# A chunked mLSTM stage worked by single heads, and by pairs of heads in row and column groups of TensorE

## The chip, the cores and the metric

The kernel runs on one core of one Trainium2 chip. The metric is the device time of one execution in microseconds; three runs of the kernel before are shown, and one further execution was profiled. The engines are TensorE (PE, with its weight loads shown apart as PEld), VectorE (DVE), ScalarE (ACT), GpSimd (POOL) and SyncE (SP). TensorE's granted clock is shown as a share of 2.4 GHz, so 0.50 is 1.2 GHz.

## The reference, cut to what matters

The whole kernel is a small network: adaptive normalisation, a token mixer (an mLSTM in both directions beside a convolution), mixture-of-experts layers, attention and a state-space part. The change touches one stage, the recurrent part of the mLSTM. For each chunk of 128 tokens, each direction and each of 4 heads (key width 64, value width 128) it computes

```
# boundary states, one chunk after the other
C_new = a * C + e * (w * v)^T k            # n is carried as a 129th column of v
# outputs of a chunk
s   = (q k^T) * exp(log_d - m_t)           # log_d is -inf above (or below) the diagonal
num = s v + e_int * (C q)
den = sum(s) + e_int * (n q)
h   = num / max(|den|, exp(-m_t))
```

There are 10 chunks in each direction: 2 of context, of which only the states are wanted, and 8 of the sequence. The two directions' h are added.

## The kernel before, in words

`stage_gates` leaves, for each of the 80 columns (10 chunks j, 2 directions d, 4 heads h), the gate sums and maxima as 128-token columns (`E`, `EI`, `EN`, `WS`, `EA`) and the negated running maxima turned to rows in `NMT` (80 x 128). Then `stage_mlstm` runs as one block, between two barriers of all engines. Its work list is `units`, one unit for each (j, d, h), 80 in all. All but the last 8 move a state (72 units), and all but the first 16 give an output (64 units, numbered v).

For one unit with an output the engines do this:

- POOL (L793): `wv`, the values weighted by `WS`, two buffers.
- TensorE, in this order: the local state (L821, `k_tok` 64 columns wide, into PSUM partitions 0-63 or 64-127 by the head's parity, banks 4 and 5 in turn), the state's product with q (L830, contraction over 64 rows), the value product (L833, 128 x 128 by 129), and then for the unit two further on the scores q k^T (L804, 64 rows) and a one-hot product that spreads that unit's row of `NMT` over all partitions (L808, 80 rows).
- DVE: for the unit one further on, `dec` = that spread row + `E` + mask (L864) and, after ACT's exponential, `pt` = scores x `dec` (L871); for this unit the sum `hsum` of the two products (L883), three instructions on one column for the denominator (L886, L888, L889), the scaled output (L894, or L896 where it is added to the other direction's) and the state's update (L900).
- ACT: the exponential (L842) and `inter`, the state's product scaled by `EI` (L852).

All operands are fp32. Each fp32 matmul shows in the trace as two loads and two matmul records. The order on each engine is the order in which the code is written; semaphores between the engines are waited for in that order. The waits that the change touches are these lines:

```
if u >= 2:
    pe.wait_ge(state_moved, u - 1)      # before the local product of unit u: two banks
...
if v >= 2:
    pe.wait_ge(pt_ready, v - 1)         # before scores(v), which run two units ahead
```

Of the kernel before, what the change touches and what calls it, by code (L numbers as in the profile page):

```python
# [108 lines left out]
def sem(s, name):  # L109
    s.sems.append(s.nc.alloc_semaphore(name))  # L110
    return s.sems[-1]
# [643 lines left out]
def stage_mlstm(s):  # L755


    nc = s.nc
    units = [(j, d, h) for j in range(STEPS) for d in range(2) for h in range(H1)]
    U0 = NC * 2 * H1  # L760
    US = (STEPS - 1) * 2 * H1
    NV = len(units) - U0
    W = DV + 1
    s.h = s.x[:, 0:NT // 2, :].rearrange("p t (a n) -> p (t a) n", a=2)
    out_unit = lambda v: units[U0 + v]
    tile_of = lambda j, d: bwd_tile(j) if d else fwd_tile(j)
    with nc.sbuf_tensor("neg_mask", [P, 2, P], F32) as neg_mask, \
            nc.sbuf_tensor("dec", [P, 2, P], F32) as dec, nc.sbuf_tensor("pt", [P, 2, P], F32) as pt, \
            nc.sbuf_tensor("wv", [P, 2, W], F32) as wv, nc.sbuf_tensor("c_state", [P, 2, 2, W], F32) as state, \
            nc.sbuf_tensor("inter", [P, 2, W], F32) as inter, nc.sbuf_tensor("hsum", [P, 2, W], F32) as hsum, \  # L770
            nc.sbuf_tensor("dn", [P, 2, 2], F32) as dn:
        masks_set, scores_done, dec_ready, exp_ready, pt_ready = (sem(s, f"m_{x}") for x in ("masks_set", "scores_done", "dec_ready", "exp_ready", "pt_ready"))
        wv_ready, local_done, state_moved = (sem(s, f"m_{x}") for x in ("wv_ready", "local_done", "state_moved"))
        num_done, inter_ready, combined = (sem(s, f"m_{x}") for x in ("num_done", "inter_ready", "combined"))

        def lanes(h):
            return slice((h % 2) * DK, (h % 2) * DK + DK)

        with nc.Block() as block:
            @block.gpsimd  # L780
            def _(pool):
                c = s.pool_c
                c.link(pool, pool.memset(neg_mask[:, :, :], 0.0))

                pool.affine_select(out=neg_mask[:, 0, :], in_=neg_mask[:, 0, :], compare_op=ALU.is_ge, fill=NEG,
                                   base=0, pattern=[[1, P]], channel_multiplier=-1).then_inc(masks_set, 1)
                pool.affine_select(out=neg_mask[:, 1, :], in_=neg_mask[:, 1, :], compare_op=ALU.is_ge, fill=NEG,
                                   base=0, pattern=[[-1, P]], channel_multiplier=1).then_inc(masks_set, 1)
                for u, (j, d, h) in enumerate(units):
                    if u < US:  # L790
                        if u >= 2:
                            pool.wait_ge(local_done, u - 1)
                        pool.tensor_scalar(wv[:, u % 2, :], s.v_aug[:, tile_of(j, d), h, :], s.WS[:, j, d, h:h + 1],  # L793
                                           None, ALU.mult).then_inc(wv_ready, 1)

            @block.tensor
            def _(pe):
                def scores(v):
                    j, d, h = out_unit(v)
                    t0 = tile_of(j, d) * P  # L800
                    if v >= 2:
                        pe.wait_ge(pt_ready, v - 1)
                    bank = s.bank[v % 2]
                    pe.matmul(bank[:, 0:P], s.qkT[lanes(h), 2 + h // 2, t0:t0 + P], s.qkT[lanes(h), h // 2, t0:t0 + P],  # L804
                              start=True, stop=True)
                    r = (j * 2 + d) * H1 + h

                    pe.matmul(bank[:, P:2 * P], s.ident[0:NCOL, r:r + 1].to_broadcast([NCOL, P]), s.NMT[:, :],  # L808
                              start=True, stop=True).then_inc(scores_done, 1)

                for u, (j, d, h) in enumerate(units):
                    v = u - U0
                    if v == -2:
                        scores(0)
                    if v == -1:
                        scores(1)
                    if u < US:
                        pe.wait_ge(wv_ready, u + 1)
                        if u >= 2:
                            pe.wait_ge(state_moved, u - 1)  # L820
                        pe.matmul(s.bank[4 + u % 2][lanes(h), 0:W], s.k_tok[:, tile_of(j, d), h * DK:(h + 1) * DK],  # L821
                                  wv[:, u % 2, :], start=True, stop=True).then_inc(local_done, 1)
                    if v >= 0:
                        t0 = tile_of(j, d) * P
                        bank = s.bank[2 + v % 2]
                        if v >= 2:
                            pe.wait_ge(combined, v - 1)

                        pe.wait_ge(state_moved, u - 2 * H1 + 1)
                        pe.matmul(bank[:, 256:256 + W], s.qkT[lanes(h), h // 2, t0:t0 + P], state[lanes(h), d, h // 2, :],  # L830
                                  start=True, stop=True)
                        pe.wait_ge(pt_ready, v + 1)
                        pe.matmul(bank[:, 0:W], pt[:, v % 2, :], s.v_aug[:, tile_of(j, d), h, :],  # L833
                                  start=True, stop=True).then_inc(num_done, 1)
                        if v + 2 < NV:
                            scores(v + 2)

            @block.scalar
            def _(act):
                def exp(v):  # L840
                    act.wait_ge(dec_ready, v + 1)
                    act.activation(dec[:, v % 2, :], dec[:, v % 2, :], ACT.Exp).then_inc(exp_ready, 1)  # L842

                for u, (j, d, h) in enumerate(units):
                    v = u - U0
                    if 0 <= v + 1 < NV:
                        exp(v + 1)
                    if v >= 0:
                        act.wait_ge(num_done, v + 1)
                        if v >= 2:  # L850
                            act.wait_ge(combined, v - 1)
                        act.activation(inter[:, v % 2, :], s.bank[2 + v % 2][:, 256:256 + W], ACT.Copy,  # L852
                                       scale=s.EI[:, j, d, h:h + 1]).then_inc(inter_ready, 1)

            @block.vector
            def _(dve):
                c = s.dve_c
                c.link(dve, dve.memset(state[:, :, :, :], 0.0))
                dve.wait_ge(masks_set, 2)

                def decay(v):
                    j, d, h = out_unit(v)
                    dve.wait_ge(scores_done, v + 1)
                    dve.scalar_tensor_tensor(dec[:, v % 2, :], s.bank[v % 2][:, P:2 * P], s.E[:, j, d, h:h + 1],  # L864
                                             neg_mask[:, d, :], ALU.add, ALU.add).then_inc(dec_ready, 1)

                def weights(v):
                    dve.wait_ge(exp_ready, v + 1)
                    if v >= 2:
                        dve.wait_ge(num_done, v - 1)  # L870
                    dve.tensor_tensor(pt[:, v % 2, :], s.bank[v % 2][:, 0:P], dec[:, v % 2, :], ALU.mult).then_inc(pt_ready, 1)  # L871

                for u, (j, d, h) in enumerate(units):
                    v = u - U0
                    if 0 <= v + 1 < NV:
                        decay(v + 1)
                    if 0 <= v + 1 < NV:
                        weights(v + 1)
                    if v >= 0:
                        dve.wait_ge(inter_ready, v + 1)  # L880
                        H = hsum[:, v % 2, :]

                        dve.tensor_tensor(H, s.bank[2 + v % 2][:, 0:W], inter[:, v % 2, :], ALU.add).then_inc(combined, 1)  # L883
                        dve.wait_ge(combined, v + 1)

                        c.link(dve, dve.tensor_scalar(dn[:, v % 2, 0:1], H[:, DV:W], -1.0, s.EN[:, j, d, h:h + 1],  # L886
                                                      ALU.mult, ALU.max))
                        c.link(dve, dve.tensor_tensor(dn[:, v % 2, 0:1], dn[:, v % 2, 0:1], H[:, DV:W], ALU.max))  # L888
                        c.link(dve, dve.reciprocal(dn[:, v % 2, 1:2], dn[:, v % 2, 0:1]))  # L889
                        t = tile_of(j, d)  # L890
                        to = s.h[:, t, h * DV:(h + 1) * DV]
                        first = j < (bwd_tile(t) if not d else t + NC)
                        if first:
                            c.then(dve.tensor_scalar(to, H[:, 0:DV], dn[:, v % 2, 1:2], None, ALU.mult))  # L894
                        else:
                            c.then(dve.scalar_tensor_tensor(to, H[:, 0:DV], dn[:, v % 2, 1:2], to, ALU.mult, ALU.add))  # L896
                    if u < US:
                        dve.wait_ge(local_done, u + 1)
                        C = state[lanes(h), d, h // 2, :]
                        dve.scalar_tensor_tensor(C, C, s.EA[lanes(h), j, d, h:h + 1], s.bank[4 + u % 2][lanes(h), 0:W],  # L900
                                                 ALU.mult, ALU.add).then_inc(state_moved, 1)


# [2263 lines left out]
```

## Time and profile before

| | |
|---|---|
| three runs | 3322.37, 3321.8, 3315.33 us; median 3321.8 |
| the profiled execution | 3317.97 us, of which the span is 3316.2 us |
| the stage's first product and last output | 453.05 us and 685.79 us after the span's start |
| mean granted clock over the span | 0.904 |

A time in the trace is counted from the span's start. A line such as `562.35 0.80 PE L830 MATMUL ... x2` gives the start, the stretch that the records cover, the engine, the line of the kernel and the number of records. What follows in brackets is idle time of that engine just before, and what ended it. Matmuls are pipelined and their ends are modelled, so the spacing of starts tells more than the durations.

### The profile page before, as it was taken

How to read it: one execution, taken by the hardware profiler on the slowest of the kernel's cores; microseconds unless marked ns; L12 is line 12 of the kernel's file. 1: busy time of each engine (PE TensorE's matmuls, PEld its weight loads, DVE VectorE, ACT ScalarE, POOL GpSimd, SP SyncE). 2: the span in 40 equal slices, each digit the busy share in tenths (PEclk: the TensorE clock that was granted, in tenths of full speed). 3: DMA queues.
4: the chain of work that ended last, by engine and by line, in shares of the span. 5: the costliest groups of instructions: out<-in, count | busy, mean ns of one | idle time of the engine just before them, and what ended most of it. 6: DMA issues, size and time to landing. Idle time of an engine off the chain costs nothing. (4 is left out here: it accounts for less than half of the span.)

```text
span 3316.2 us, 39108 instructions
## 1 busy us (share of the span) xinstructions
PE 2861.8 (86%) x12086; PEld 2025.9 (61%) x12087; DVE 1726.0 (52%) x2710; ACT 1168.1 (35%) x1598; POOL 840.4 (25%) x1036
## 2 busy tenths in 40 slices
PE   4999969968787999999999993998987999883897
PEld 4455446647536777777777772446664666673776
DVE  3667845556535556756666554036644111435653
ACT  1100011123205556656666553005513111213653
POOL 0100021122173333333343332038320000103333
PEclk9999955569798999999999996999998999986999
DMA  5321100003316878978888865300011111316873
GB/s 217 103 102 54 54 0 1 1 29 142 152 65 226 276 225 271 316 252 300 306 274 295 249 165 168 113 0 1 27 15 51 38 44 33 135 70 223 306 232 59
DMA packets 159184, 463.49 MB, mean 140 GB/s; under 512 B 37964, under 2 KB 67264, under 8 KB 138328
## 3 DMA queue, kind: packets, MB, share of 16 engines
q1 hardware_dynamic: 115816, 358.12, 29.2%
q0 software_dynamic: 43264, 104.02, 13.1%
q8 instruction: 60, 0.98, 0.1%
q14 instruction: 44, 0.36, 0.0%
HBM read 414.31 MB, written 91.62 MB: 153 GB/s over the span
## 5 line engine op out<-in xcount | busy, mean ns | idle before, releaser
L1829 DVE TENSOR_TENSOR moe_low<-moe_raw,moe_high 128x2048 fp32r<-128x2048 f32 x160 | 359.5, 2288 | 80.6 <-ACT moe_high L1774 80.6
L1739 PE MATMUL psum<-moe_high,moe_xg_high 128*128 128x512 f32 x960 | 389.9, 406 | 6.1 <-issue 3.1
L1741 PE MATMUL psum<-moe_high,moe_xg_low 128*128 128x512 f32 x960 | 378.3, 394 | 0.0
L1740 PE MATMUL psum<-moe_low,moe_xg_high 128*128 128x512 f32 x960 | 375.5, 391 | 0.0
L1774 ACT ACTIVATE moe_high<-moe_raw 128x2048 fp32r<-128x2048 f32 x160 | 297.5, 1914 | 0.1
L1675 POOL DMA_INDIRECT moe_acc<-moe_y_blk,moe_is_now x97 | 216.2, 2229 | 303.6 <-DMA moe_acc<-moe_y_blk,moe_is_now 273.0
L1786 ACT ACTIVATE moe_y_blk<-psum,row_w 128x1024 f32 x124 | 138.1, 1113 | 232.7 <-DMA moe_acc<-moe_y_blk,moe_is_now 129.1
L1726 PE MATMUL psum<-moe_high_down,moe_hid_high 128*128 x488 | 208.3, 427 | 12.7 <-DVE moe_hid_low L1838 12.6
L1713 PE MATMUL psum<-ident,moe_xg 128*128 128x128 f32 x976 | 132.5, 280 | 96.8 <-DMA moe_xg<-moe_rows,moe_ig_now 96.8
L1739 PEld LDWEIGHTS psum<-moe_high,moe_xg_high 128*128 128x128 f32 x960 | 181.7, 189 | 43.1 <-issue 4.8
L1741 PEld LDWEIGHTS psum<-moe_high,moe_xg_low 128*128 128x128 f32 x960 | 180.8, 188 | 43.1
L1740 PEld LDWEIGHTS psum<-moe_low,moe_xg_high 128*128 128x128 f32 x960 | 181.7, 189 | 36.0
L1834 DVE TENSOR_TENSOR moe_xg_low<-psum,moe_xg_high 128x512 fp32r<-128x512 f32 x244 | 157.4, 685 | 82.6 <-ACT moe_xg_high L1780 82.4
L1728 PE MATMUL psum<-moe_high_down,moe_hid_low 128*128 x488 | 196.6, 403 | 0.0
L1727 PE MATMUL psum<-moe_low,moe_hid_high 128*128 x488 | 196.3, 402 | 0.0
L1713 PEld LDWEIGHTS psum<-ident,moe_xg 128*128 128x128 f32 x976 | 111.6, 143 | 128.6 <-DMA moe_xg<-moe_rows,moe_ig_now 119.9
L1829 DVE TENSOR_TENSOR moe_low<-moe_raw,moe_high_down 128x2048 fp32r<-128x2048 f32 x80 | 182.7, 2284 | 0.0
L2300 PE MATMUL psum<-w_ring,hT 128*128 128x512 f32 x384 | 167.1, 598 | 9.2 <-DMA w_ring<-in_w_in 9.2
L502 PE MATMUL psum<-hT,w_ring 128*128 128x512 f32 x384 | 168.8, 599 | 1.1 <-PEq L344 1.1
L1780 ACT ACTIVATE moe_xg_high<-psum 128x512 fp32r<-128x512 f32 x244 | 133.3, 596 | 85.2 <-PE psum L1713 81.4
L1838 DVE TENSOR_TENSOR moe_hid_low<-psum,moe_hid_high 128x256 fp32r<-128x256 f32 x122 | 51.2, 420 | 210.7 <-ACT moe_hid_high L1791 210.6
L1665 POOL DMA_INDIRECT moe_xg<-moe_rows,moe_ig_now x122 | 132.6, 1087 | 107.4 <-POOL moe_ig_now L1662 99.9
(574 smaller groups left out, 5305.3 us busy)
## 6 DMA issues: line engine op xcount, KB each, us to landing
moe_raw<-in_we_gate SPq DMA_DIRECT2D x64, 1024.0 KB, 7.7
moe_raw<-in_we_up SPq DMA_DIRECT2D x64, 1024.0 KB, 11.4
moe_raw<-in_we_down SPq DMA_DIRECT2D x64, 1024.0 KB, 7.5
moe_raw<-in_w_e_gate SPq DMA_DIRECT2D x16, 1024.0 KB, 7.0
moe_raw<-in_w_e_up SPq DMA_DIRECT2D x16, 1024.0 KB, 10.1
moe_raw<-in_w_e_down SPq DMA_DIRECT2D x16, 1024.0 KB, 8.7
w_ring<-in_w_in SPq DMA_DIRECT2D x12, 1024.0 KB, 7.3
wada<-in_w_ada SPq DMA_DIRECT2D x8, 1024.0 KB, 10.5
```

Source lines behind the costliest of these rows:

```text
L502: last = pe.matmul(bank[:, 0:width], w[:, k, c0:c0 + P], h[:, k, :], start=(k == 0), stop=(k == KD - 1))
L1675: pool.indirect_dma_start(mo.acc, bass.IndirectOffsetOnAxis(ap=is_now[q][:, 0:1], axis=0), y_blk[:, q * D:(q + 1) * D], None, bounds_check ...
L1713: last = pe.transpose(bx[k // 4][:, (k % 4) * P:(k % 4 + 1) * P], xg[:, k * P:(k + 1) * P], s.ident[:, :])
L1726: pe.matmul(by[n][:, :], R(hid_high[:, f, :]), w_hi, start=(f == 0), stop=False)
L1727: pe.matmul(by[n][:, :], R(hid_high[:, f, :]), w_lo, start=False, stop=False)
L1728: last = pe.matmul(by[n][:, :], R(hid_low[:, f, :]), w_hi, start=False, stop=(f == KF - 1))
L1739: pe.matmul(to, x_hi, R(of_k(w_hi, k)), start=(k == 0), stop=False)
L1740: pe.matmul(to, x_hi, R(of_k(w_lo, k)), start=False, stop=False)
L1741: last = pe.matmul(to, x_lo, R(of_k(w_hi, k)), start=False, stop=(k == KD - 1))
L1774: act.activation(R(high[:, at:at + 2048]), raw[r][:, part], ACT.Copy).then_inc(w_high, 1)
L1829: dve.tensor_tensor(R(low[:, at:at + 2048]), raw[r][:, part], hi, ALU.subtract).then_inc(w_low, 1)
L2300: last = pe.matmul(s.bank[i % 4], s.hT[:, k, t * P:(t + 1) * P], ring[:, g % 2, k, :], start=(k == 0), stop=(k == KD - 1))
```

## The change

The work list becomes `pairs`: one entry for each (j, d, k), where k stands for heads 2k and 2k+1, 40 in all; 36 move states (`PS`) and 32 give outputs (`NV`, numbered v from pair `P0` = 8 on). For a pair TensorE issues two local products into the two halves of one bank (bank 7), two products with the state from rows 0-63 and 64-127 into two banks, two value products, and two score products likewise from the two row halves. The spread of the maxima is made once for two pairs (`maxima(g)`: one matmul, 80 rows by 512 columns, from a table `NM4` that holds `NMT` four times, each with the rows of one head alone). The chain of DVE and ACT is widened: one mask addition of 512 columns for four heads, one `pt` of 256, one `hsum` of 258, denominators of 2 columns, one state update of 128 partitions; `E` goes into the exponential as its bias. Scores run one pair ahead, where they ran two units ahead.

```
-    units = [(j, d, h) for j in range(STEPS) for d in range(2) for h in range(H1)]
+    pairs = [(j, d, k) for j in range(STEPS) for d in range(2) for k in range(H1 // 2)]
+    P0 = NC * H1
+    PS = (STEPS - 1) * H1
+    NV = len(pairs) - P0
...
+        both = lambda first: s.psum[:, first * 512:(first + 2) * 512].rearrange("p (i n) -> p i n", i=2)
+        out_banks = lambda v: 2 + 2 * (v % 2)
...
+                for p, (j, d, k) in enumerate(pairs[:PS]):
+                    if p >= 2:
+                        pool.wait_ge(local_done, p - 1)
+                    for i in range(2):
+                        h = 2 * k + i
+                        pool.tensor_scalar(wv[:, p % 2, i, :], s.v_aug[:, tile_of(j, d), h, :], s.WS[:, j, d, h:h + 1],
                                            None, ALU.mult).then_inc(wv_ready, 1)
...
+                def maxima(g):
+
+                    pe.matmul(s.bank[6][:, :], of_group[:, NC * 2 + g:NC * 2 + g + 1].to_broadcast([NCOL, P]), NM4[:, :, :],
+                              start=True, stop=True).then_inc(maxima_done, 1)
+
                 def scores(v):
...
-                    if v >= 2:
-                        pe.wait_ge(pt_ready, v - 1)
...
+                    for i in range(2):
+                        last = pe.matmul(s.bank[i][:, 0:P], s.qkT[lanes(i), 2 + k, t0:t0 + P], s.qkT[lanes(i), k, t0:t0 + P],
+                                         start=True, stop=True)
+                    last.then_inc(scores_done, 1)
+
+                for p, (j, d, k) in enumerate(pairs):
+                    v = p - P0
+                    if v == -1:
+                        pe.wait_ge(maxima_set, 1)
+                        maxima(0)
                         scores(0)
...
+                    if p < PS:
+                        pe.wait_ge(wv_ready, 2 * (p + 1))
+                        if p >= 1:
+                            pe.wait_ge(state_moved, p)
+                        for i in range(2):
+                            h = 2 * k + i
+                            last = pe.matmul(s.bank[7][lanes(i), 0:W], s.k_tok[:, tile_of(j, d), h * DK:(h + 1) * DK],
+                                             wv[:, p % 2, i, :], start=True, stop=True)
+                        last.then_inc(local_done, 1)
                     if v >= 0:
...
+                        pe.wait_ge(state_moved, p - H1 + 1)
+                        for i in range(2):
+                            pe.matmul(s.bank[bank + i][:, 256:256 + W], s.qkT[lanes(i), k, t0:t0 + P], state[lanes(i), d, k, :],
+                                      start=True, stop=True)
                         pe.wait_ge(pt_ready, v + 1)
...
+                        for i in range(2):
+                            last = pe.matmul(s.bank[bank + i][:, 0:W], pt[:, v % 2, i, :], s.v_aug[:, tile_of(j, d), 2 * k + i, :],
+                                             start=True, stop=True)
+                        last.then_inc(num_done, 1)
+                        if v + 1 < NV:
+                            scores(v + 1)
+                        if v % 2 == 0 and v + 2 < NV:
+                            pe.wait_ge(masked, v // 2 + 1)
+                            maxima(v // 2 + 1)
...
+                def exps(g):
+                    j, d, _ = pairs[P0 + 2 * g]
+                    act.wait_ge(masked, g + 1)
+                    for h in range(H1):
+                        one = decay[:, g % 2, h, :]
+                        act.activation(one, one, ACT.Exp, bias=s.E[:, j, d, h:h + 1]).then_inc(exp_ready, 1)
...
+                for p, (j, d, k) in enumerate(pairs):
+                    v = p - P0
+                    if v % 2 == 1 and 0 <= v + 1 < NV:
+                        mask((v + 1) // 2)
                     if 0 <= v + 1 < NV:
                         weights(v + 1)
                     if v >= 0:
...
+                        dve.tensor_tensor(H, both(out_banks(v))[:, :, 0:W], inter[:, v % 2, :, :], ALU.add).then_inc(combined, 1)
...
+                    if p < PS:
+                        dve.wait_ge(local_done, p + 1)
+                        C = state[:, d, k, :]
+                        dve.scalar_tensor_tensor(C, C, EA2[:, j, d, k:k + 1], s.bank[7][:, 0:W],
                                                  ALU.mult, ALU.add).then_inc(state_moved, 1)
```

On TensorE, in the middle of the stage, the round of one unit was this (five products; `waits` names the semaphores):

```order
L821 MATMUL psum<-wv,k_tok 64x129 [waits m_state_moved,m_wv_ready]
L830 MATMUL psum<-c_state,qkT 128x129 [waits m_state_moved,m_combined]
L833 MATMUL psum<-v_aug,pt 128x129 [waits m_pt_ready]
L804 MATMUL psum<-qkT 128x128 [waits m_pt_ready]
L808 MATMUL psum<-NMT,ident 128x128
```

The same place in the changed kernel, one pair that also issues `maxima`:

```order
L824 MATMUL psum<-wv,k_tok 64x129 [waits m_state_moved,m_wv_ready]
L824 MATMUL psum<-wv,k_tok 64x129
L833 MATMUL psum<-c_state,qkT 128x129 [waits m_state_moved,m_combined]
L833 MATMUL psum<-c_state,qkT 128x129
L837 MATMUL psum<-v_aug,pt 128x129 [waits m_pt_ready]
L837 MATMUL psum<-v_aug,pt 128x129
L808 MATMUL psum<-qkT 128x128 x2
L801 MATMUL psum<-NM,of_group 128x512 [waits m_masked]
```

Two products of one kind now stand next to each other, and the spread of the maxima (L808 before, L801 now) stands behind every second pair's scores.

On DVE the round of one unit was this:

```order
L864 SCALAR_TENSOR_TENSOR dec<-psum,E,neg_mask 128x128 [waits m_scores_done]
L871 TENSOR_TENSOR pt<-psum,dec 128x128 [waits m_num_done,m_exp_ready]
L883 TENSOR_TENSOR hsum<-psum,inter 128x129 [waits m_inter_ready]
L886 TENSOR_SCALAR dn<-hsum,EN 128x1 [waits m_combined]
L888 TENSOR_TENSOR dn<-dn,hsum 128x1 [waits dve_own]
L889 RECIPROCAL dn<-dn 128x1 [waits dve_own]
L894 TENSOR_SCALAR x<-hsum,dn 128x128 [waits dve_own]
L900 SCALAR_TENSOR_TENSOR c_state<-c_state,EA,psum 64x129 [waits m_local_done]
```

The changed kernel's round of one pair, with the mask addition that every second pair has:

```order
L887 TENSOR_TENSOR decay<-psum,neg_mask 128x512 [waits m_maxima_done]
L896 TENSOR_TENSOR pt<-psum,decay 128x256 [waits m_num_done,m_scores_done,m_exp_ready]
L908 TENSOR_TENSOR hsum<-psum,inter 128x258 [waits m_inter_ready]
L911 SCALAR_TENSOR_TENSOR dn<-hsum,EN 128x2 [waits m_combined]
L912 TENSOR_TENSOR dn<-dn,hsum 128x2 [waits dve_own]
L913 RECIPROCAL dn<-dn 128x2 [waits dve_own]
L920 TENSOR_SCALAR x<-hsum,dn 128x128 [waits dve_own]
L920 TENSOR_SCALAR x<-hsum,dn 128x128
L926 SCALAR_TENSOR_TENSOR c_state<-c_state,EA,psum 128x129 [waits m_local_done]
```

The wait for the scores moved from the mask addition to `pt`, and the state's update stays the last instruction of the round.

## Rows read from the trace of the kernel before

**Rows 1.** Work by window, middle of the stage: PE, PEld, DVE, ACT, POOL, clock, DMA, GB/s.

```profile
470.00:560.00 90.00, 90.00 (x257) 58.43 (x256) 51.63 (x205) 17.27 (x51) 15.89 (x26) 0.50 0.00 1
```

**Rows 2.** Timeline, TensorE, one unit's round and the next's first product.

```profile
562.35 0.80 PE L830 MATMUL psum<-c_state,qkT 64*128 64x129 f32 x2
...
563.08 0.80 PE L833 MATMUL psum<-v_aug,pt 128*128 128x129 f32 x2
...
563.81 0.79 PE L804 MATMUL psum<-qkT 64*128 64x128 f32 x2
...
564.53 0.79 PE L808 MATMUL psum<-NMT,ident 80*128 80x128 f32 x2
...
565.26 0.69 PE L821 MATMUL psum<-wv,k_tok 128*64 128x129 f32 x2
...
565.88 0.80 PE L830 MATMUL psum<-c_state,qkT 64*128 64x129 f32 x2
```

**Rows 3.** Timeline, the stage's last output.

```profile
685.79 0.35 DVE L896 SCALAR_TENSOR_TENSOR x<-hsum,dn,x 128x128 f32<-128x128 f32 x1
```

**Rows 4.** Timeline, TensorE at 1.2 GHz, in the gates' stage: two like products in a row.

```profile
432.83 0.64 PE L690 MATMUL psum<-g_FG,tri_ge 128*128 128x80 f32 x2
...
433.25 0.63 PE L691 MATMUL psum<-g_FG,ones 128*128 128x80 f32 x2
```

**Rows 5.** Timeline and window (as rows 1), later stage: 64-row products from both halves.

```profile
2482.93 3.31 PEld L2759 LDWEIGHTS psum<-x,ssm_R 64*128 64x128 f32 x30 [12.17 <-issue]
...
2482.90:2486.20 3.30, 3.24 (x30) 3.27 (x32) 3.30 (x2) 0.00 (x0) 0.98 (x1) 0.50 0.02 5
```

**Rows 6.** Timeline, a later stage at 2.4 GHz: products into alternate column halves.

```profile
2455.30 7.21 PE L2739 MATMUL psum<-ssm_UT,ssm_WT 128*64 128x128 f32 x128 [1.06 <-ACT ssm_WT L2861]
```

**Rows 7.** Timeline, DVE, the end of one round and the next round.

```profile
561.76 0.29 DVE L894 TENSOR_SCALAR x<-hsum,dn 128x128 f32<-128x128 f32 x1
561.96 0.34 DVE L900 SCALAR_TENSOR_TENSOR c_state<-c_state,EA,psum 64x129 f32<-64x129 f32 x1
...
563.92 0.37 ACT L852 ACTIVATE inter<-psum,EI 128x129 f32<-128x129 f32 x1 [1.01 <-PE psum L833]
564.32 0.29 DVE L883 TENSOR_TENSOR hsum<-psum,inter 128x129 f32<-128x129 f32 x1 [1.09 <-ACT inter L852]
...
564.65 0.21 DVE L886 TENSOR_SCALAR dn<-hsum,EN 128x1 f32<-128x1 f32 x1
...
565.29 0.29 DVE L894 TENSOR_SCALAR x<-hsum,dn 128x128 f32<-128x128 f32 x1
565.61 0.35 DVE L900 SCALAR_TENSOR_TENSOR c_state<-c_state,EA,psum 64x129 f32<-64x129 f32 x1
```

**Rows 8.** Groups by form: busy us, mean ns of one, idle before.

```profile
L1834 DVE TENSOR_TENSOR moe_xg_low<-psum,moe_xg_high 128x512 fp32r<-128x512 f32 x244 | 157.4, 685 | 82.6 <-ACT moe_xg_high L1780 82.4
...
L2812 DVE TENSOR_TENSOR x<-psum,x 128x256 f32<-128x256 f32 x8 | 3.4, 424 | 5.7 <-PE psum L2739 4.1 <-POOL ssm_R L2688 1.6
...
L793 POOL TENSOR_SCALAR wv<-v_aug,WS 128x129 f32<-128x129 f32 x72 | 43.9, 611 | 165.8 <-PE psum L821 158.6 <-issue 7.3
```

**Rows 9.** Timeline, the stage's first states.

```profile
453.05 1.29 PE L821 MATMUL psum<-wv,k_tok 128*64 128x129 f32 x4 [10.05 <-POOL wv L793]
...
453.88 0.34 DVE L900 SCALAR_TENSOR_TENSOR c_state<-c_state,EA,psum 64x129 f32<-64x129 f32 x1 [9.35 <-PE psum L821]
```

**Rows 10.** Timeline, loads for 512-column products in the stage behind; a window as in rows 1.

```profile
686.44 0.50 PEld L931 LDWEIGHTS psum<-conv_y,ones 128*128 128x128 f32 x2 [2.36 <-issue]
687.46 0.34 PEld L931 LDWEIGHTS psum<-conv_y,ones 128*128 128x128 f32 x1 [0.52 <-issue]
688.31 0.34 PEld L931 LDWEIGHTS psum<-conv_y,ones 128*128 128x128 f32 x1 [0.52 <-issue]
...
690.00:700.00 10.00, 8.55 (x20) 3.52 (x19) 4.92 (x9) 4.20 (x8) 10.00 (x7) 1.00 0.00 0
```

More of the change, by code:

```diff
@@ L823, in _ @@
                     if v >= 0:
[L824 to L825 removed]
+                        t0, bank = tile_of(j, d) * P, out_banks(v)
                         if v >= 2:
                             pe.wait_ge(combined, v - 1)
[L829 to L831 removed]
+                        pe.wait_ge(state_moved, p - H1 + 1)
@@ new lines, in _ @@
+                exps(0)
+                for v in range(NV):
+                    j, d, k = pairs[P0 + v]
+                    if v % 2 == 1 and v + 1 < NV:
+                        exps(v // 2 + 1)
+                    act.wait_ge(num_done, v + 1)
+                    if v >= 2:
+                        act.wait_ge(combined, v - 1)
+                    for i in range(2):
+                        h = 2 * k + i
+                        act.activation(inter[:, v % 2, i, :], s.bank[out_banks(v) + i][:, 256:256 + W], ACT.Copy,
@@ L857, in _ @@
                 c = s.dve_c
-                c.link(dve, dve.memset(state[:, :, :, :], 0.0))
-                dve.wait_ge(masks_set, 2)
-                def decay(v):
-                    j, d, h = out_unit(v)
+                heads = lambda i: s.EA[lanes(i), :, :, :].rearrange("p j d (k i) -> p (j d k) i", i=2)[:, :, i]
+                unit = s.ident[0:NCOL, 0:NCOL]
+                c.then(dve.memset(state[:, :, :, :], 0.0))
+                for i in range(2):
+                    c.then(dve.tensor_copy(EA2[lanes(i), :, :, :].rearrange("p j d k -> p (j d k)"), heads(i)))
@@ new lines, in _ @@
+                c.then(dve.tensor_reduce(of_group[:, :], unit.rearrange("p (g h) -> p g h", h=H1), AX_X, ALU.add))
+                c.link(dve, dve.tensor_reduce(of_head[:, :], unit.rearrange("p (g h) -> p h g", h=H1), AX_X, ALU.add))
+                for h in range(H1):
+                    c.then(dve.tensor_scalar(NM4[:, h, :], s.NMT[:, :], of_head[:, h:h + 1], None, ALU.mult))
+                c.wait(dve)
+                dve.sem_inc(maxima_set, 1)
+                dve.wait_ge(masks_set, 2)
@@ L867, in weights @@
-                def weights(v):
-                    dve.wait_ge(exp_ready, v + 1)
                     if v >= 2:
                         dve.wait_ge(num_done, v - 1)
[L871 to L876, printed above, removed]
+                    dve.tensor_tensor(pt[:, v % 2, :, :], both(0)[:, :, 0:P], decay[:, v // 2 % 2, 2 * k:2 * k + 2, :],
+                                      ALU.mult).then_inc(pt_ready, 1)
@@ L897, in _ @@
[L897 to L900, printed above, removed]
+                        for i in range(2):
+                            h = 2 * k + i
+                            to = s.h[:, t, h * DV:(h + 1) * DV]
+                            if first:
+                                c.then(dve.tensor_scalar(to, H[:, i, 0:DV], D2[:, i, 1:2], None, ALU.mult))
+                            else:
+                                c.then(dve.scalar_tensor_tensor(to, H[:, i, 0:DV], D2[:, i, 1:2], to, ALU.mult, ALU.add))
```

90 lines of the change are left out of this document (24 added, 66 removed).

## The prediction, made before the changed kernel had run

> **What bounds the kernel now.** I read the busy work by window first, then the timeline of one round, then who waits for whom inside it. Through the middle of the stage TensorE is busy without a gap, at a granted clock of 0.50, while DVE works 57% of the time and the transfers are nearly nil [rows 1]. The round of one unit, from one L830 to the next, is 565.88 - 562.35 = 3.53 us [rows 2]. It consists of five products whose starts stand 0.73, 0.73, 0.72, 0.73 and 0.62 us apart; the last, the local state with 64 weight columns, is the short one. DVE's wait for ACT (1.09 us before L883) and ACT's for TensorE are slack in the same round [rows 7]. So TensorE's issue sets the stage, and the stage lasts from 453.05 to 685.79 + 0.35 = 686.14 us [rows 9, 3]. It stands between two barriers, and all of it is on the path: what it gains the kernel gains.
>
> Why 0.73? Products of 512 columns follow at 0.85 us a pass [rows 10], so 128 columns are 0.213 us a pass and 0.43 us for the two passes. Two like products in a row stand 0.42 apart [rows 4]. So a product that follows one of another kind pays about 0.30 us more, every one of the five. The Trainium skill (TensorEngine Tiling (Array Packing), Tiling Modes, Key Properties) says that changing the tiling mode drains TensorE. By that rule the 0.30 stays once for each change of kind, which speaks against counting the whole stage as halved; the rows' 0.73 against 0.42 agree.
>
> **What a pair costs on TensorE.** The trace has pairs like the new ones. Sixty-four-row products from the two halves, at clock 0.50, load weights at 3.31 / 30 = 0.110 us each, so four loads, a pair, take 0.44 us: both members pass side by side [rows 5]. Products into the two column halves, at clock 1.00, make 128 records in 7.21 us, 0.056 a record and 0.225 a pair, where streams of 128 columns at that clock are 0.213 for one product alone (half of 0.43) [rows 6, 10]. I therefore price a pair as one product plus a few hundredths. The skill (TensorE: Matmul & The Clock Gate, Part 3) gives about 4 ns for each further member; priced that way my sum would be some 0.07 us a pair smaller, and no run here shows that number.
>
> - Local pair: 0.62 + 0.01 = 0.63 us (before: 2 x 0.62).
> - State product pair: 0.73 + 0.03 = 0.76 (before 2 x 0.73).
> - Value products: both use the whole array, so they can't pass side by side, but they are now alike and in a row: 0.73 + 0.43 = 1.16.
> - Score pair, to the end of its second member's records: 0.76 + 0.07 = 0.83.
>
> Together 3.38 us from the local pair's start to the scores' end, where two rounds took 7.06. The 64 spreads (L808) become `maxima`, once for two pairs. At 512 columns its first pass takes 687.46 - 686.44 = 1.02, the second 0.85, and 0.13 until the next kind can load (0.73 - 0.38 - 0.21): 2.0 us, bounded by 1.7 (two passes) and 2.4.
>
> **What is late next.** With 3.38 us, TensorE is no longer alone. Before, the local product had two banks and scores ran two units ahead, so DVE's round lay beside TensorE's. Now the local pair of p+1 waits for the state's update of p, because bank 7 is the only one; that update is the last instruction of DVE's round; and the round begins with `pt` for the next pair, which waits for scores that TensorE issues last. So each pair is a ring: TensorE's four steps, then DVE's whole round, then TensorE again. DVE's part, after the scores' end:
>
> - handover from TensorE: 0.04 to 0.14. ACT to DVE is 0.03 (563.92 + 0.37 to 564.32) [rows 7]; the first L900 starts 0.14 after the end of the product it waited for [rows 9]. `pt` now has three waits, so I take 0.14.
> - `pt`, 256 columns: an instruction of 256 columns from PSUM lasts 0.424 [rows 8]; the next can start some 0.09 before an instruction's end (L894 lasts 0.29, L900 starts 0.20 after it) [rows 7]: 0.34.
> - `hsum`, 258 columns, then a wait for its own end: 0.42 + 0.04 = 0.46. Its `inter` operands are two ACT instructions of 0.37 that start after the value products and end before the scores do; hidden by the score pair, with about 0.4 us to spare.
> - three narrow ones: 565.29 - 564.65 = 0.64 [rows 7]. The first becomes another form, for two columns; from none to 0.05 more; I take 0.65.
> - two outputs of 128 columns: 2 x 0.20, bounded by 2 x 0.32, since L894 to L900 shows both spacings (561.76 to 561.96, 565.29 to 565.61) [rows 7]. From v = 16 on the adding form lasts 0.35 and not 0.29 [rows 3, 7], 0.14 a pair more.
> - state, 128 partitions but the same 129 columns: 0.35, and 0.05 to TensorE.
>
> Sum 2.39 us (bounds 2.2 and 2.7). The ring is 3.38 + 2.39 = 5.77 us, 5.91 from v = 16 on, against 7.06: 18% less, not the half.
>
> Beside the ring: the mask addition, 0.69 for 512 columns [rows 8], runs in every second pair right behind the state, and four exponentials behind it are ready some 1.7 us into TensorE's 3.38. `maxima` starts behind the scores' drain and ends 0.76 + 2.0 = 2.76 us after their start; DVE's state arrives at 0.83 + 2.39 = 3.2. So it lies in the gap where TensorE waits anyway, with 0.4 us cover; without cover it would cost up to 2.0 us in each of 14 pairs, 28 us. POOL needs 2 x 0.61 a pair [rows 8], hidden in the ring. The small new work ahead (copies, reductions, four 80 x 128 products on DVE) lies before 453.05, where TensorE waited 10.05 us for POOL [rows 9]: nothing.
>
> **The sum.** The first local pair needs the second `wv` too: 453.05 + 0.60 = 453.65. The pairs without output are POOL's, 1.21 each; the seventh starts at 460.9. Then `maxima` (2.0), scores (0.76), the eighth local pair at about 464.9 with its state behind the first `pt`: the ninth local pair, that of v = 0, at 465.75. Then 16 x 5.77 + 12 x 5.91 = 163.2 us, to 629.0. The last four pairs have no state update to wait for; ring scores, `pt`, value products, about 2.6 us each and one exposed `maxima` (2.0): the last output ends at 640.8. That is 686.14 - 640.8 = 45 us less. Against the profiled execution, 3317.97 - 45.3 = 3272.7 us. The three runs' median is 3321.8, 3.8 us above that execution; the median of the changed kernel I put at 3321.8 - 45.3 = 3276 us.
>
> **The rivals.**
> - *The pairs don't pass side by side and each member pays its drain* (the slower end). If products from the other half of the rows count as a change of kind, the local pair is 1.24, state pair 1.45, scores 1.52: TensorE's part 5.37, the ring 7.76, above 7.06. It turns slower than before once TensorE's part is over 4.67. Cost against the forecast 1.99 x 28 = 56 and about 6 ahead and behind: 3338 us. Against it: rows 5 and 6. For it: both show long runs of one kind, never one lone pair between others. 7%.
> - *They pass one after the other without a drain between*: local 1.05, state 1.16, scores 1.23, ring 6.98: 1.21 x 28 + 3 = 37 us above the forecast, 3313. 5%.
> - *`maxima` or DVE is longer than its cover*: the ring's upper bounds, 0.3 x 32 = 10 us, and up to 28 for an exposed `maxima`: 3286 to 3304. 12%.
> - *The granted clock rises.* Then TensorE's passes, 0.43 + 0.43 + 0.86 + 0.43 = 2.15 us of the ring, halve: 28 x 1.07 = 30 us less, 3246; for some pairs only, 3260. For it: 512-column products in a row brought the clock to 1.00 [rows 10], and `maxima` is one such. The skill (TensorE: Matmul & The Clock Gate, Why this matters for your kernels) says that a TensorE kept continuously busy gets the full clock; by that it would have had it before. The row says otherwise, 90.00 of 90.00 us busy at 0.50 [rows 1], and now it gets idler. 8%.
>
> **How the numbers follow.** The forecast, a ring of TensorE and DVE with packed pairs, has 68%: 3276 us, 3268 to 3286 by its bounds. Range for 8 in 10: 3254 to 3302. It takes in most of the third and fourth rival and leaves the first two out. Differences within 0.2%, 6.6 us, are what a measurement of this kernel can't tell from no change: same 0.04. Slower 0.07, which is the first rival. Faster 0.89.
>
> **What would show it.** Right: the starts of consecutive local pairs 5.8 us apart, TensorE idle about 1.9 us before each local pair with DVE's state as the releaser (nearly none where `maxima` stands between), state pair to value product 0.76, value to scores 1.16, clock 0.50 throughout, last output near 641. Wrong: members of a pair starting 0.4 or 0.7 apart instead of hundredths; a `maxima` that ends after the state; a clock of 1.00 within the stage; or a local pair that doesn't wait for the state.

## The result, and the profile after

| | before | changed |
|---|---|---|
| median of four runs | 3321.07 us | 3271.14 us |
| lowest and highest | 3315.33 to 3322.37 | 3266.35 to 3277.35 |
| ratio | | 0.9854, 95% interval 0.9834 to 0.9874 |
| stage, first local product to the end of the last output | 233.1 us | 184.9 us |

The ratio is 48 us less, 42 to 55 by its interval; the forecast was 45 us less (3276 us). The stage alone gives 48.2 us. The two profiled executions differ by only 41 us (3317.97 and 3277.35 us), because the program behind the stage, which nothing changed, took 2630.1 us in the one before and 2637.1 us in the changed one. It moves as much or more in the experiments: 2626.2, 2626.5 and 2631.0 us in three traces from one chip, but 2661.9 us in a fourth from there, of a kernel that leaves out most of the maxima. The stage is therefore read from its own start and end.

The experiments ran on two other occasions: on a chip where the kernel before had a median of 3352.07 us (update early, members apart, no `maxima`, two banks), and on one where it had 3322.94 us (the other four). Whole kernels are therefore compared by their ratio to the kernel before on the same chip. Two executions, each the profiled one of its kernel, were in a slow state and stand outside all ratios: one of the kernel with the members apart, 5723.29 us, and one of the kernel with two banks, 3443.84 us, whose trace is used for the stage alone, where its clock was 0.50 as in the others.

The window in the middle of the stage, columns as in [rows 1]:

```profile
470.00:560.00 90.00, 67.99 (x272) 39.77 (x270) 35.75 (x134) 20.25 (x64) 19.22 (x32) 0.50 0.00 1
```

TensorE was busy for all 90 us before; now for 68, at the same granted clock. Two rounds in the timeline (start, stretch in us, engine, line; weight loads left out) answer to [rows 2, 7]:

```profile
539.69 0.70 PE L824 MATMUL psum<-wv,k_tok 128*64 128x129 f32 x4 [0.38 <-DVE c_state L926]
...
540.32 0.80 PE L833 MATMUL psum<-c_state,qkT 64*128 64x129 f32 x4
...
541.05 1.23 PE L837 MATMUL psum<-v_aug,pt 128*128 128x129 f32 x4
...
542.21 0.80 PE L808 MATMUL psum<-qkT 64*128 64x128 f32 x4
542.32 0.63 ACT L865 ACTIVATE inter<-psum,EI 128x129 f32<-128x129 f32 x2 [0.86 <-PE psum L837]
543.12 0.43 DVE L896 TENSOR_TENSOR pt<-psum,decay 128x256 f32<-128x256 f32 x1 [2.97 <-issue]
543.46 0.42 DVE L908 TENSOR_TENSOR hsum<-psum,inter 128x258 f32<-128x258 f32 x1
543.91 0.16 DVE L911 SCALAR_TENSOR_TENSOR dn<-hsum,EN 128x2 f32<-128x2 f32 x1
...
544.50 0.48 DVE L920 TENSOR_SCALAR x<-hsum,dn 128x128 f32<-128x128 f32 x2
544.90 0.34 DVE L926 SCALAR_TENSOR_TENSOR c_state<-c_state,EA,psum 128x129 f32<-128x129 f32 x1
...
545.39 0.70 PE L824 MATMUL psum<-wv,k_tok 128*64 128x129 f32 x4 [2.38 <-DVE c_state L926]
...
547.90 0.80 PE L808 MATMUL psum<-qkT 64*128 64x128 f32 x4
...
548.63 2.07 PE L801 MATMUL psum<-NM,of_group 80*128 80x512 f32 x2
...
551.08 0.70 PE L824 MATMUL psum<-wv,k_tok 128*64 128x129 f32 x4 [0.37 <-DVE c_state L926]
```

The starts of the local pairs stand 5.70 and 5.69 us apart, where two rounds took 7.06. Each local pair is released by DVE's state update, and four records of a pair cover 0.70 or 0.80 us, as two records of one product did. TensorE's idle time in front of it is 2.38 us; where `maxima` stands between, 0.37.

### The profile page after: what moved, and what is told of

Read it like the earlier page. It is cut to its first block and busy times, and to the rows that moved or that the text cites. A ratio compares the mean times of both kernels' runs of the same rounds, so it can differ in the third digit from the quotient of the medians.

```text
span 3275.2 us, 38552 instructions
## 1 busy us (share of the span) xinstructions
PE 2775.4 (85%) x11990; PEld 1960.3 (60%) x11991; DVE 1672.7 (51%) x2474; ACT 1165.4 (36%) x1598; POOL 834.7 (25%) x1036
## 5 line engine op out<-in xcount | busy, mean ns | idle before, releaser
L1752 PE MATMUL psum<-moe_high_down,moe_hid_high 128*128 x488 | 207.9, 426 | 11.9 <-DVE moe_hid_low L1864 11.4
```

The costliest lines, as they stand in the source:

```text
L1752: pe.matmul(by[n][:, :], R(hid_high[:, f, :]), w_hi, start=(f == 0), stop=False)
```

## The experiments

Each is an edit of the changed kernel. "Stage" is always the first local product's start to the last output's end, read from the experiment's own trace. Each stage time comes from one trace. The spacing of the pairs repeats to 0.01 us within a trace, and it is the same in the changed kernel and in the one without `maxima`, which was traced on another occasion (5.69 and 5.83 us in both), while the rest of the program moves by several microseconds; so the stage tells most.

**The state's update earlier in DVE's round.**

```
                     if 0 <= v + 1 < NV:
                         weights(v + 1)
+                    if p < PS:
+                        dve.wait_ge(local_done, p + 1)
+                        C = state[:, d, k, :]
+                        dve.scalar_tensor_tensor(C, C, EA2[:, j, d, k:k + 1], s.bank[7][:, 0:W],
+                                                 ALU.mult, ALU.add).then_inc(state_moved, 1)
                     if v >= 0:
                         dve.wait_ge(inter_ready, 2 * (v + 1))
...
-                    if p < PS:
-                        dve.wait_ge(local_done, p + 1)
-                        C = state[:, d, k, :]
-                        dve.scalar_tensor_tensor(C, C, EA2[:, j, d, k:k + 1], s.bank[7][:, 0:W],
-                                                 ALU.mult, ALU.add).then_inc(state_moved, 1)
```

> The changed kernel with one move on DVE: the state's update stands right behind pt and ahead of hsum, the denominators and the outputs. Changed kernel: a pair takes 5.69 us, the stage (first local product to last output) 184.9 us. Theory (a ring of TensorE and DVE's whole round): hsum 0.45, the narrow three 0.59 and the outputs 0.40 to 0.54 leave the ring. Pairs without maxima fall to 0.63 + 0.76 + 1.16 + 0.80 + 0.86 = 4.2 us; in those with maxima (2.0) TensorE itself is then the later one, 5.3 us; mean 4.75, stage shorter by 28 x 0.95 = 26 us, whole kernel about 3244. Rival (TensorE's products set the pair and the idle time before the local pair only fills up what the order leaves): stage unchanged, about 3271.

Measured: stage 158.45 us; local pairs 4.25 and 5.25 us apart in turn. The ratio to the kernel before is 0.9771 (0.9755 to 0.9787), against 0.9854. The timeline of this kernel (columns as above):

```profile
521.51 0.80 PE L808 MATMUL psum<-qkT 64*128 64x128 f32 x4
...
522.42 0.42 DVE L896 TENSOR_TENSOR pt<-psum,decay 128x256 f32<-128x256 f32 x1 [2.53 <-issue]
522.76 0.34 DVE L908 SCALAR_TENSOR_TENSOR c_state<-c_state,EA,psum 128x129 f32<-128x129 f32 x1
523.01 0.42 DVE L913 TENSOR_TENSOR hsum<-psum,inter 128x258 f32<-128x258 f32 x1
523.24 0.70 PE L824 MATMUL psum<-wv,k_tok 128*64 128x129 f32 x4 [0.93 <-DVE c_state L908]
...
526.49 2.07 PE L801 MATMUL psum<-NM,of_group 80*128 80x512 f32 x2
...
528.49 0.70 PE L824 MATMUL psum<-wv,k_tok 128*64 128x129 f32 x4
```

`hsum` and all behind it now lie beside TensorE's work: the idle time before the local pair fell from 2.38 to 0.93 us, and behind `maxima` there is none. Not one instruction was removed, only one moved, and 26.5 us of the stage went. So TensorE did wait for DVE's whole round, and the rival (an unchanged stage) is refuted.

**The members of a pair apart.**

```
+                def local(i):
+                    h = 2 * k + i
+                    last = pe.matmul(s.bank[7][lanes(i), 0:W], s.k_tok[:, tile_of(j, d), h * DK:(h + 1) * DK],
+                                     wv[:, p % 2, i, :], start=True, stop=True)
+                    if i == 1:
+                        last.then_inc(local_done, 1)
...
-                        for i in range(2):
-                            h = 2 * k + i
-                            last = pe.matmul(s.bank[7][lanes(i), 0:W], s.k_tok[:, tile_of(j, d), h * DK:(h + 1) * DK],
-                                             wv[:, p % 2, i, :], start=True, stop=True)
-                        last.then_inc(local_done, 1)
+                        for i in range(2 if v < 0 else 0):
+                            local(i)
...
                         for i in range(2):
+                            if p < PS:
+                                local(i)
                             pe.matmul(s.bank[bank + i][:, 256:256 + W], s.qkT[lanes(i), k, t0:t0 + P], state[lanes(i), d, k, :],
                                       start=True, stop=True)
```

> The changed kernel with the two local and the two state products no longer adjacent: local 0, state 0, local 1, state 1. Same instructions, same waits ahead of the four. Theory (members side by side only when adjacent, and each change of kind pays 0.30): 0.63 + 0.76 become 2 x 0.62 + 2 x 0.73 = 2.70, 1.31 us more in each of 28 pairs, stage 184.9 + 37 = 222 us, kernel about 3308: over two thirds of the gain is gone. Rival (the gain is from fewer and wider instructions on DVE and ACT and the shared spread of the maxima, not from the groups of the array): no more than a few us.

Measured: ratio to before 0.9949 (0.9929 to 0.9968), against 0.9854 with the members adjacent. The same kernel ran once more for its trace.

> The same kernel as e2_apart (local 0, state 0, local 1, state 1), for a trace at clock 0.50: the profiled execution of e2_apart was a disturbed one. Theory (adjacent members pass side by side, each change of kind pays 0.30): a pair 5.69 + 1.31 = 7.0 us, 7.13 from v = 16 on, stage 222 us. Rival: the pair stays within 0.3 us of 5.69.

Measured: stage 220.2 us; pairs 6.95 us apart, 7.09 from v = 16 on. TensorE in this kernel:

```profile
541.19 0.66 PE L814 MATMUL psum<-wv,k_tok 128*64 128x129 f32 x2 [0.33 <-issue]
...
541.79 0.80 PE L839 MATMUL psum<-c_state,qkT 64*128 64x129 f32 x2
...
542.51 0.69 PE L814 MATMUL psum<-wv,k_tok 128*64 128x129 f32 x2
...
543.13 0.79 PE L839 MATMUL psum<-c_state,qkT 64*128 64x129 f32 x2
...
543.86 1.23 PE L843 MATMUL psum<-v_aug,pt 128*128 128x129 f32 x4
```

From the first local product to the value products it is 2.67 us, where adjacent pairs took 541.05 - 539.69 = 1.36. So 1.31 us a pair is what adjacency is worth for two of the four kinds, as expected, and 35.3 us of the stage: most of what the change gained. Width on DVE and ACT alone would not have done it. The edit takes away two things at once, the passing side by side and two changes of kind saved; no run separates them. By the 0.30 us of the prediction the changes would be 0.6 of the 1.31, an estimate.

**`maxima` left out.**

```
-                        if v % 2 == 0 and v + 2 < NV:
-                            pe.wait_ge(masked, v // 2 + 1)
-                            maxima(v // 2 + 1)
...
-                    dve.wait_ge(maxima_done, g + 1)
+                    dve.wait_ge(maxima_done, 1)
```

> The changed kernel with maxima issued once, for the first two pairs, and left out for the other fifteen, whose masks are added to the first one's result: the decay of later chunks is computed from wrong maxima. 15 x 2.0 = 30 us of TensorE work is gone. Theory (maxima lies in the gap where TensorE waits for the state): the 14 in the ring give nothing, the one in the last pairs about 2 us; stage 183 us. Rival (maxima delays the local pair or the mask): up to 28 us shorter.

Measured: stage 183.8 us against 184.9; the pairs stay 5.69 to 5.71 and 5.83 us apart, also where `maxima` was. Thirty microseconds of TensorE work were free but for 1.1, since they lay in the wait for DVE. The 1.1 us lie behind the last local pair: from its start to the last output it takes 16.1 us and not 17.2. (The one execution took 3331.66 us, with 2694.2 us behind the stage; only the stage is compared.) The wait only grew, in 470 to 600 us (waiter, releaser: us in total, times, longest), first the changed kernel, then this one:

```profile
PE psum L824 <- DVE c_state L926: 31.6, 23, 2.5
```

```profile
PE psum L824 <- DVE c_state L923: 55.6, 23, 2.5
```

**A second bank for the local products.**

```
-                        if p >= 1:
-                            pe.wait_ge(state_moved, p)
+                        if p >= 2:
+                            pe.wait_ge(state_moved, p - 1)
...
-                            last = pe.matmul(s.bank[7][lanes(i), 0:W], s.k_tok[:, tile_of(j, d), h * DK:(h + 1) * DK],
+                            last = pe.matmul(s.bank[p % 2][lanes(i), 0:W], s.k_tok[:, tile_of(j, d), h * DK:(h + 1) * DK],
...
+                    if v >= 2:
+                        pe.wait_ge(combined, v - 1)
                     for i in range(2):
-                        last = pe.matmul(s.bank[i][:, 0:P], s.qkT[lanes(i), 2 + k, t0:t0 + P], s.qkT[lanes(i), k, t0:t0 + P],
+                        last = pe.matmul(s.bank[out_banks(v) + i][:, 384:512], s.qkT[lanes(i), 2 + k, t0:t0 + P], s.qkT[lanes(i), k, t0:t0 + P],
...
-                        if v >= 2:
-                            pe.wait_ge(combined, v - 1)
                         pe.wait_ge(state_moved, p - H1 + 1)
+                        pe.wait_ge(pt_ready, v + 1)
```

DVE's reads follow: `pt` from columns 384 to 511 of the output banks, the state's update from bank `p % 2`.

> The changed kernel with two banks for the local products: the scores go into free columns of the output banks, which frees banks 0 and 1; the local pair of p+1 waits for the state of p-1 and no longer of p, and the wait for pt stands ahead of the state products. Theory (ring): broken, TensorE alone sets the pair: 0.63 + 0.76 + 1.16 + 0.73 = 3.28 and 2.0 for maxima in every second, mean 4.3 us; stage shorter by 28 x 1.39 + 2 = 41 us, to 144, kernel about 3230. Rival (DVE's or ACT's own work is the bound, round after round): DVE's busy time of 2.4 to 3.0 us a pair would not allow it either way, so a pair above 4.5 us would show a wait that I don't see, such as pt behind the state products.

Measured: stage 148.1 us, 36.8 less than in the changed kernel; pairs 3.25 and 5.36 us apart in turn, mean 4.3; ratio to before 0.9744 (0.9724 to 0.9764), which against 0.9854 is 36.5 us, so that whole kernels and stage agree. The middle of the stage:

```profile
510.00:600.00 90.00, 89.27 (x359) 51.92 (x357) 47.36 (x170) 26.62 (x84) 26.84 (x45) 0.50 0.00 1
```

TensorE is busy again, 89.27 of 90 us. The pairs came as worked out; the stage fell by 37 and not 41 us. What is missing lies at the stage's end. From the last local pair's start to the last output this kernel takes 19.7 us and the changed kernel 17.2, where it should have been shorter. The wait for `pt` stands ahead of the state products here, and there is no local pair left to cover it; three times among the last pairs TensorE stands still for `pt`:

```profile
640.12 0.80 PE L810 MATMUL psum<-qkT 64*128 64x128 f32 x4
...
641.02 0.42 DVE L896 TENSOR_TENSOR pt<-psum,decay 128x256 f32<-128x256 f32 x1 [1.99 <-PE psum L810]
...
641.59 0.80 PE L834 MATMUL psum<-c_state,qkT 64*128 64x129 f32 x4 [0.67 <-DVE pt L896]
```

From scores to state products it is 1.47 us. In the changed kernel, where the state products need not wait for `pt`, it was 0.58.

**The same two cuts together: two banks, no `maxima`.**

> The kernel of e4_two_banks (pairs 3.25 and 5.36 us in turn, stage 148.1) with maxima issued once, and left out for the other fifteen, whose masks are added to the first one's result: wrong maxima for later chunks. Theory (with the ring broken TensorE is the bound and maxima is on the path): each of 14 pairs in the middle falls from 5.36 to 3.25, stage 148 - 31 = 117 us, where the same cut in the changed kernel gave 1 us. Rival (DVE's round takes its place): DVE needs 2.3 to 3.0 us a pair, so a pair of 3.25 can stand; a pair above 3.4 would show it.

Measured: stage 123.7 us, 24.5 less than with two banks alone, where the same cut had given 1.1 us in the changed kernel. So whether `maxima` costs anything is decided by the ring. But the stage is 7 us longer than the 117 expected: the pairs are 3.37 and 3.54 us apart (3.37 and 3.67 from v = 16 on), not 3.25, and the rival holds in part. In this kernel TensorE waits for `pt` again, longest in every second pair:

```profile
524.09 0.69 DVE L884 TENSOR_TENSOR decay<-psum,neg_mask 128x512 f32<-128x512 f32 x1
...
524.80 1.28 ACT L850 ACTIVATE decay<-decay,E 128x128 f32<-128x128 f32 x4 [3.12 <-DVE decay L884]
...
525.53 0.42 DVE L893 TENSOR_TENSOR pt<-psum,decay 128x256 f32<-128x256 f32 x1 [0.76 <-ACT decay L850]
...
526.10 0.80 PE L834 MATMUL psum<-c_state,qkT 64*128 64x129 f32 x4 [0.36 <-DVE pt L893]
```

The mask addition stands behind the last state update on DVE, ACT's exponentials behind it, and `pt` behind those. That is the next bound: it holds the pairs at 3.46 us on average, later 3.52, where TensorE alone would take 3.25.

**The order of scores and value products.**

```
                         pe.wait_ge(pt_ready, v + 1)
+                        if v + 1 < NV:
+                            scores(v + 1)
                         for i in range(2):
                             last = pe.matmul(s.bank[bank + i][:, 0:W], pt[:, v % 2, i, :], s.v_aug[:, tile_of(j, d), 2 * k + i, :],
                                              start=True, stop=True)
                         last.then_inc(num_done, 1)
-                        if v + 1 < NV:
-                            scores(v + 1)
```

> The changed kernel with the next pair's scores right behind the state products and ahead of this pair's value products. Theory (ring): scores then follow products of their own kind, so one change of kind (0.30 us) goes and pt of the next pair is early; but hsum must now wait for the value products' end and for ACT's inter (0.04 + 0.63) behind them, which the scores used to hide. Ring: 0.63 + 0.39 + 0.76 + 1.23 + 0.67 + 0.04 + 0.45 + 0.59 + 0.40 + 0.40 = 5.55 us against 5.69, stage shorter by 4 us, kernel ratio about 0.984. Rival (the order value first, scores behind, is what makes the stage fast, since the scores cover inter): pair longer than 5.69.

Measured: stage 182.5 us; pairs 5.65 us apart, 5.79 from v = 16 on; ratio to before 0.9848 (0.9823 to 0.9872), which can't be told from the changed kernel's. One round:

```profile
539.07 0.64 PE L808 MATMUL psum<-qkT 64*128 64x128 f32 x4
539.63 1.23 PE L839 MATMUL psum<-v_aug,pt 128*128 128x129 f32 x4
...
540.90 0.63 ACT L865 ACTIVATE inter<-psum,EI 128x129 f32<-128x129 f32 x2 [1.29 <-PE psum L839]
541.56 0.43 DVE L908 TENSOR_TENSOR hsum<-psum,inter 128x258 f32<-128x258 f32 x1 [1.33 <-ACT inter L865]
...
543.50 0.70 PE L824 MATMUL psum<-wv,k_tok 128*64 128x129 f32 x4 [2.64 <-DVE c_state L926]
```

TensorE saves one change of kind, and DVE gives it back by waiting for `inter`, which the scores used to cover. The theory had 5.55: from `hsum` to the next local pair it is 543.50 - 541.56 = 1.94 us where I had put 1.84. "Value first, scores behind" as such is worth nothing to speak of in either direction.

**Both, the ring broken and the scores first.** The diff is against the kernel with two banks.

```
                             pe.matmul(s.bank[bank + i][:, 256:256 + W], s.qkT[lanes(i), k, t0:t0 + P], state[lanes(i), d, k, :],
                                       start=True, stop=True)
+                        if v + 1 < NV:
+                            scores(v + 1)
                         for i in range(2):
...
                         last.then_inc(num_done, 1)
-                        if v + 1 < NV:
-                            scores(v + 1)
```

> The kernel of e4_two_banks with the next pair's scores right behind the state products and ahead of the value products. Theory (TensorE is the bound, each change of kind pays 0.30): state products to scores falls from 0.76 to 0.39, one change of kind less a pair: pairs 2.9 and 5.0, mean 3.95, stage shorter by 28 x 0.36 = 10 us, to 138. Rival: hsum of the pair before is late for the bank that the scores write, or pt is late, and TensorE waits for DVE; then no gain.

Measured: stage 131.4 us, the shortest of the kernels that leave nothing out; median 3220.64 us where the kernel before had 3322.94, ratio 0.97 (0.9676 to 0.9724). Most pairs are 2.95 and 4.84 us apart, 0.30 and 0.52 less than with two banks alone, where 0.36 was expected. One pair with `maxima`:

```profile
472.97 0.80 PE L834 MATMUL psum<-c_state,qkT 64*128 64x129 f32 x4
...
473.59 0.80 PE L810 MATMUL psum<-qkT 64*128 64x128 f32 x4
...
474.32 1.23 PE L839 MATMUL psum<-v_aug,pt 128*128 128x129 f32 x4
...
475.34 1.92 PE L801 MATMUL psum<-NM,of_group 80*128 80x512 f32 x2
...
477.18 0.70 PE L826 MATMUL psum<-wv,k_tok 128*64 128x129 f32 x4
```

The order saves more than the one change of kind that was expected. `maxima`, with 80 rows, now stands behind the value products, with 128 rows, and that is no change of kind either: it starts 1.02 us behind them, where the scores (64 rows) start 1.16 us behind them in the other kernels, and 1.84 us later the local pair starts, where it was 2.00. Two changes, 0.6 us, go in these pairs, and 0.11 that TensorE waited for `pt` with two banks alone. Of that 0.19 is lost again, since the scores wait for the bank that `hsum` of the pair before has to clear: `hsum` ends at 473.54, the scores start at 473.59, and from state to value products it is 1.35 us where the pairs without `maxima` take 1.16. That is the rival of the expectation, in small.

With the mean of 3.9 us the stage would be about 137 us. Of the other 5.4 us, 2.0 lie behind the last local pair (17.65 us to the last output, not 19.67), and 3.3 come with a granted clock that rose to 1.00, 2.4 GHz, for three short stretches. One of them:

```profile
520.00:560.00 40.00, 37.77 (x176) 22.57 (x175) 25.80 (x91) 13.16 (x42) 12.02 (x20) 0.59 0.01 1
...
540.12 0.70 PE L826 MATMUL psum<-wv,k_tok 128*64 128x129 f32 x4
540.75 0.80 PE L834 MATMUL psum<-c_state,qkT 64*128 64x129 f32 x4
...
542.36 1.02 PE L801 MATMUL psum<-NM,of_group 80*128 80x512 f32 x2
...
543.31 0.44 PE L826 MATMUL psum<-wv,k_tok 128*64 128x129 f32 x4
...
545.42 0.44 PE L826 MATMUL psum<-wv,k_tok 128*64 128x129 f32 x4 [0.38 <-DVE c_state L926]
...
547.20 0.49 PE L834 MATMUL psum<-c_state,qkT 64*128 64x129 f32 x4 [1.34 <-DVE pt L896]
```

After the rise `maxima` takes 1.02 and not 2.07 us, and local pairs are 543.31 - 540.12 = 3.19 and 545.42 - 543.31 = 2.11 us apart. The following pair takes 6.36 us, since TensorE outruns DVE (it waits 1.34 us for `pt`): three pairs in 11.66 us instead of 4.84 + 2.95 + 4.84 = 12.63. By its ratio this kernel is ahead of the one with two banks alone (0.9744) and of the one with the update early (0.9771).

## Why the prediction was right

- *The ring.* Forecast 5.77 and 5.91 us, measured 5.69 and 5.83. The idle time before the local pair names the state's update as its releaser, and moving or unlinking that update shortened the stage by 26.5 and 36.8 us.
- *TensorE's part.* 3.38 forecast; 0.63 + 0.73 + 1.16 + 0.80 = 3.32 measured. The two row pairs were 0.03 us each too dear: the members start 0.007 us apart inside the stage, not the 0.03 that I had taken. The value products' 1.16 is 0.73 + 0.43, as priced; the two like products of [rows 4] are no support for the 0.43, since they have 80 columns and not 128. The first two rivals (members not side by side) are out, and the run with the members apart shows what they would have cost.
- *DVE's part.* 2.39 forecast, 545.39 - 543.01 = 2.38 measured. Handover 0.11 (0.14 taken), the narrow three 0.59 (0.65 taken: the new two-column form lasts 0.16, the one-column form before 0.21), the step from state to TensorE 0.15 instead of 0.05.
- *Cover of `maxima`.* 0.4 us forecast, 0.37 measured as the idle time that is left, and its removal gave 1.1 us of 30. So the third rival is out too. One sign did not fit the prediction's own sum: TensorE idle about 1.9 us before a local pair, where the sum has 2.39 from the scores' end; measured 2.38.
- *The start* of v = 0's local pair: 465.75 forecast, 465.66 measured. That is luck, since two errors cancel. The first local pair came at 453.17 and not 453.65, the eighth at 464.01 and not 464.9, and the step to the ninth was 1.65 us where 0.85 was taken: `pt` is held up by ACT's exponentials there, and the state's update stands behind it. POOL does not set the first pairs either; each is released by DVE's state update, 1.23 us apart (the second 1.32).
- *The last four pairs*: 11.8 forecast, 11.4 measured, though four rings of 2.6 and a `maxima` of 2.0 would add up to 12.4. What was not foreseen there: the state products follow the scores after 0.58 and not 0.73 us. Both are 64-row products, and behind each other they are no change of kind:

```profile
633.09 0.80 PE L808 MATMUL psum<-qkT 64*128 64x128 f32 x4
...
633.67 0.64 PE L833 MATMUL psum<-c_state,qkT 64*128 64x129 f32 x4
```

- *The clock* stayed at 0.50 through the stage, as forecast. The rival can't be dismissed for this stage, though: in the last experiment the clock did rise.

The forecast was 3 us short of the stage's gain, of which 2.2 are 28 rounds at 0.08 us. The mechanism came as forecast, and the rounds, which make up nearly all of the gain, were right within 0.1 us in each part and not only in their sum.

## What to carry to other kernels

When small matmuls are packed side by side, count the changes of kind as well as the columns: like products belong next to each other, and a run of them costs one change, about 0.30 us here. What counts as like was the part of the array that is used, not the operands: state products and scores (64 rows each) were alike, and so were value products and `maxima` (128 and 80 rows). Then ask what the shorter TensorE round is chained to. Here a single PSUM bank, released by the last instruction of DVE's round, kept back 37 us beside the 48 that were gained, and moving one instruction returned 26 of them. Work that is shown to be free inside such a wait gets its price back as soon as the wait is gone, so judge it again after every step.

## What the runs showed of the hardware that was not expected

The granted clock rose in one order of the products and not in others that kept TensorE as busy. It stayed at 0.50 through the stage in the kernel before, which was busy all the time, in the changed kernel, with pairs 5.7 us apart and TensorE 76% busy, and in the kernel with two banks, busy 89.27 of 90 us. With two banks and the scores behind the state products TensorE was busy all the time at 0.50 from 469 us on, and then the clock stood at 1.00 in three stretches of the stage, near 500, 514 and 545 us. The stretch before the first rise, and the first:

```profile
469.00:497.00 28.00, 28.00 (x129) 17.51 (x128) 16.70 (x61) 9.50 (x30) 8.87 (x15) 0.50 0.00 1
497.00:504.00 7.00, 4.89 (x40) 3.15 (x38) 5.04 (x19) 2.41 (x8) 3.10 (x6) 0.99 0.00 0
```

The busy time in the records doesn't tell these kernels apart. Which property of the order it was, these runs, one trace of each kernel, don't show.
